# Attention's two heads as pairs of half-array products, in a two-layer decoder trunk on one core

## What is computed

```python
def dilated_branch(q, k, v, rel_bias, window, dilation):      # layer 0, per query group
    ...
    scores = jnp.where(allowed[:, None], scores + bias, NEG_INF)
    m = jnp.max(scores, axis=-1)
    p = jnp.exp(scores - m[..., None])
    l = jnp.sum(p, axis=-1)
    o = jnp.einsum('bdnqhk,bdnkhc->bdnqhc', p, vv.astype(jnp.float32))
```

## Time and profile before

| | |
|---|---|
| median of 3 executions | 1723.69 us (1720.13 to 1725.03) |
| the profiled execution's own time | 1725.31 us |
| its span | 1723.5 us |
| PE busy | 1635.0 us, 95% |
| DVE busy | 1329.4 us, 77% |
| ACT busy | 1119.9 us, 65% |
| POOL busy | 53.0 us, 3% |

### The profile page before, as it was taken

One profiled execution on the slowest core, in us unless ns is written; L12 is line 12 of the kernel. 1 busy time (PEld: TensorE's weight loads), 2 busy tenths in 40 slices (PEclk: granted clock), 3 DMA queues, 4 the chain that ended last, 5 costly groups with the idle time before them and its releaser, 6 DMA issues.

```text
span 1723.5 us, 26169 instructions
## 1 busy us (share of the span) xinstructions
PE 1635.0 (95%) x8684; PEld 1372.9 (80%) x8684; DVE 1329.4 (77%) x1711; ACT 1119.9 (65%) x1498; POOL 53.0 (3%) x37
## 2 busy tenths in 40 slices
PE   7999988999988987999999999999999999999996
PEld 6899957999976765788788788788788787887885
DVE  4777665555557754898898898998998998998995
ACT  5555445334445643787777777777787788787774
POOL 1422100000000000000000000000000000000000
PEclk9999988999998988999999999999999999999999
DMA  9744324666612342899999999998999998998990
GB/s 263 198 122 122 104 86 141 189 183 183 171 37 74 110 172 74 311 378 347 331 380 325 343 372 333 334 383 328 330 386 332 331 385 319 341 384 321 343 379 29
DMA packets 272721, 442.77 MB, mean 257 GB/s; under 512 B 12496, under 2 KB 120160, under 8 KB 272672
## 3 DMA queue, kind: packets, MB, share of 16 engines
q1 hardware_dynamic: 271664, 438.47, 72.7%
q0 software_dynamic: 1008, 3.68, 1.1%
HBM read 440.28 MB, written 1.84 MB: 257 GB/s over the span
## 4 chain that ended last, share of the span: by engine, by line
PE 90%; DVE 5%; ACT 2%; DMA 2%; issue 1%; DVEq 0%; POOL 0%; ACTq 0%; POOLq 0%
PE ps L594 26%; PE ps L595 26%; PE ps L596 26%; PE ps L892 2%; PE ps L903 2%; PE ps L667 2%; DMA big<-in_even_w_in 2%; PE ps L933 1%; DVE w_lo L1253 1%; PE ps L689 1%; PE ps L665 1%; PE ps L676 1%; ACT w_hi L974 1%; PE ps L621 1%; PE ps L693 0%
## 5 line engine op out<-in xcount | busy, mean ns | idle before, releaser
L1253 DVE TENSOR_TENSOR w_lo<-big,w_hi 128x1024 fp32r<-128x1024 f32 (+1 forms) x843 | 991.5, 1216 | 247.6 <-ACT w_hi L974 156.3
L1195 ACT CAST w_hi<-big 128x1024 fp32r<-128x1024 f32 x672 | 689.8, 1056 | 142.6 <-PE ps L596 142.2
L594 PE MATMUL ps<-w_hi,m_hi 128*128 128x512 f32 (+1 forms) x1008 | 400.3, 397 | 4.9 <-DVE w_lo L1253 4.9
L596 PE MATMUL ps<-w_hi,m_lo 128*128 128x512 f32 (+1 forms) x1008 | 391.4, 388 | 0.0
L595 PE MATMUL ps<-w_lo,m_hi 128*128 128x512 f32 (+1 forms) x1008 | 391.3, 388 | 0.0
L594 PE MATMUL ps<-h_hi,w_hi 128*128 128x256 f32 (+1 forms) x824 | 240.7, 292 | 5.4 <-DVE w_lo L1253 5.4
L595 PE MATMUL ps<-h_lo,w_hi 128*128 128x256 f32 (+1 forms) x824 | 236.4, 287 | 0.0
L596 PE MATMUL ps<-h_hi,w_lo 128*128 128x256 f32 (+1 forms) x824 | 236.2, 287 | 0.0
L594 PEld LDWEIGHTS ps<-w_hi,m_hi 128*128 128x128 f32 x1008 | 190.8, 189 | 46.0 <-issue 9.5
L974 ACT CAST w_hi<-big 128x1024 fp32r<-128x1024 f32 (+1 forms) x171 | 165.4, 978 | 95.0 <-PE ps L596 82.0
L596 PEld LDWEIGHTS ps<-w_hi,m_lo 128*128 128x128 f32 x1008 | 190.7, 189 | 39.6
(11 more groups left out here) (202 smaller groups left out, 1424.7 us busy)
## 6 DMA issues: line engine op xcount, KB each, us to landing
big<-in_odd_w_gate SPq DMA_DIRECT2D x112, 1024.0 KB, 7.0
big<-in_odd_w_up SPq DMA_DIRECT2D x112, 1024.0 KB, 7.5
big<-in_odd_w_down SPq DMA_DIRECT2D x112, 1024.0 KB, 6.7
big<-in_even_w_in SPq DMA_DIRECT2D x42, 512.0 KB, 4.6
big<-in_even_w_gate SPq DMA_DIRECT2D x22, 512.0 KB, 3.9
big<-in_even_w_up SPq DMA_DIRECT2D x22, 512.0 KB, 4.0
big<-in_even_w_down SPq DMA_DIRECT2D x22, 512.0 KB, 3.7
big<-in_w_out SPq DMA_DIRECT2D x20, 512.0 KB, 4.3
```

Source lines behind the costliest of these rows:

```text
L594: mm(dst, a[0], b[0], start=start, stop=False, **kw)
L596: return mm(dst, a[1], b[0], start=False, stop=stop, **kw)
L1195: nc.scalar.copy(w_hi[:, slot, :], ring[s][:, (u % 2) * UNIT:(u % 2 + 1) * UNIT]).then_inc(s_hi, 1)
L1253: return V.tensor_tensor(dst, src, lead.bitcast(F32), ALU.subtract)
```

## The change

Both heads' score products are issued in one call, head 0 and head 1 by turns, each on its half of the array's rows (`scores(nxt)`), and both heads' V products in one call, each on its half of the columns (`mix(now)`). Head 1 gets buffers of its own: `zq` for scores (it takes the place of `qiT` and `kiT`), `selm` or `zq` for the turned probabilities, `pr` for the probabilities; its third group of scores goes to the half bank beside head 0's, and DVE reads that bank first (`third_read`), since the next pair's first projection goes there. DVE reads both heads' scores in one place of the step (`head_scores(nxt)`). The order of calls on PE, ACT and DVE is new.

```diff
-        qiT = sb("qiT", [P, 4, SEQ])
-        kiT = sb("kiT", [P, SEQ])
+        zq = sb("zq", [P, 5 * SEQ])
+        qiT = zq[:, 0:4 * SEQ].rearrange("p (c n) -> p c n", c=4)
+        kiT = zq[:, 4 * SEQ:5 * SEQ]
...
+            zs = zq if pair.nbr == NBR and hh else z
...
+        def score_columns(pair, hh, t, b0, b1):
 
             if pair.nbr == 1:
                 n0 = SEQ if pair.cross else P
-                return ps[:, hh, (0, n0)[t]:(n0, n0 + SEQ)[t]].rearrange("p (b s) -> p b s", b=1)
-            if t == 0:
-                return ps[:, 0, 0:NBR * P].rearrange("p (b s) -> p b s", b=NBR)
-            return ps[:, 1:3, :].rearrange("p k n -> p (k n)")[:, 0:NBR * SEQ].rearrange("p (b s) -> p b s", b=NBR)
+                src = ps[:, hh, (0, n0)[t]:(n0, n0 + SEQ)[t]]
+            elif t == 0:
+                src = ps[:, hh, b0 * P:b1 * P]
+            elif b1 <= 2:
+                src = ps[:, (2, 7)[hh], b0 * SEQ:b1 * SEQ]
+            else:
+                src = ps[:, pair.bank(pair.nbr), hh * SEQ:(hh + 1) * SEQ]
+            return src.rearrange("p (b s) -> p b s", b=b1 - b0)
+
+        def value_bank(pair):
+            return ps[:, 5 if pair.l == 0 else 2, 0:SEQ]
+
+        def turned(pair, hh):
+
+            return ps[:, 5 if hh == 0 or pair.kind == "even" else 0 if pair.gs[-1] == NPAIR - 1 else 7, :]
+
+        def probs(pair, hh):
+            if pair.kind == "even":
+                return (pn[:, 0:CAUSAL], pr[:, 0:CAUSAL])[hh]
+            return pr[:, 512 * hh:512 * hh + (512 if pair.cross else CAUSAL)]
+
+        def probs_turned(pair, hh):
+            second = selm[:, :] if pair.kind == "even" else zq[:, 0:512]
+            return (pts[:, :], second)[hh]
...
+                if pair.l == 0 and m == 0 and norm is None:
+                    pe.wait_ge(S["third_read"], PAIRS if pair.cross else pair.g)
...
+            def scores(pair):
+
                 S = s_at[pair.l]
                 pe.wait_ge(S["evacuated"], pair.before() + (1 if pair.cross else pair.nbr + 1))
 
-                if pair.l == 0:
-                    pe.wait_ge(S["scores_read"], 2 * pair.g + hh + 1)
-                elif not (isinstance(pair.g, int) and pair.g == 0):
-                    pe.wait_ge(S["scores_read"], 2 * pair.g + hh)
-                r = slice(HD * hh, HD * hh + HD)
+                pe.wait_ge(S["scores_read"], 2 * pair.g + 1)
                 k = keys(pair)
-                for b in range(pair.nbr):
-                    mm(score_banks(pair, hh, 0)[:, b, :], qT[r, pair.par, b, 0:P], k[r, 0:SEQ if pair.cross else P],
-                       start=True, stop=True)
-                    last = mm(score_banks(pair, hh, 1)[:, b, :], qT[r, pair.par, b, P:SEQ], k[r, :], start=True, stop=True)
-                last.then_inc(S["scores"], 1)
+                if pair.nbr == 1:
+                    turns = [[(0, 0), (1, 0)]] * 2
+                else:
+                    turns = [[(1, 2), (0, 0), (0, 1), (0, 2), (1, 0), (1, 1)], [(1, 0), (0, 0), (0, 1), (0, 2), (1, 1), (1, 2)]]
+                for i in range(len(turns[0])):
+                    for hh in range(2):
+                        t, b = turns[hh][i]
+                        r = slice(HD * hh, HD * hh + HD)
+                        if (hh, b) == (1, 2) and t:
+                            pe.wait_ge(S["third_left"], pair.g + 1)
+                        last = mm(score_columns(pair, hh, t, b, b + 1)[:, 0, :], qT[r, pair.par, b, tok(t)],
+                                  k[r, 0:SEQ if pair.cross or t else P], start=True, stop=True)
+                        if (hh, b) == (0, 2) and t:
+                            last.then_inc(S["third_left"], 1)
+                        if i == len(turns[0]) - 1:
+                            last.then_inc(S["scores"], 1)
...
-            def mix(pair, hh):
+            def mix(pair):
+
                 S = s_at[pair.l]
-                pe.wait_ge(S["probsT"], 2 * pair.g + hh + 2)
-                if hh == 0:
-                    pe.wait_ge(S["mix_lo"], pair.g + 1)
-                    if not pair.cross:
-                        pe.wait_ge(S["values"], pair.g + 1)
-                o = ps[HD * hh:HD * hh + HD, 6, :]
+                pe.wait_ge(S["probsT"], 2 * pair.g + 3)
+                pe.wait_ge(S["mix_lo"], pair.g + 1)
+                if not pair.cross:
+                    pe.wait_ge(S["values"], pair.g + 1)
                 v = (vx[:, pair.l * XPAIRS + pair.gs[0] - PAIRS, :, :] if pair.cross else vN[:, :, :])
-                v = v[:, :, HD * hh:HD * hh + HD]
-                mm(o[:, 0:SEQ], v[:, 0, :], pts[:, 0:SEQ], start=True, stop=False)
-                if pair.cross:
-                    last = mm(o[:, 0:SEQ], v[:, 1, :], pts[:, SEQ:2 * SEQ], start=False, stop=True)
-                else:
-                    last = mm(o[:, P:SEQ], v[:, 1, :], pts[:, SEQ:SEQ + P], start=False, stop=True)
-                last.then_inc(S["mixed"], 1)
+                for t in range(TT):
+                    for hh in range(2):
+                        h = slice(HD * hh, HD * hh + HD)
+                        n0 = 0 if pair.cross else P * t
+                        last = mm(ps[h, 6, n0:SEQ], v[:, t, h], probs_turned(pair, hh)[:, SEQ * t:SEQ * (t + 1) - n0],
+                                  start=(t == 0), stop=(t == TT - 1))
+                        if t == TT - 1:
+                            last.then_inc(S["mixed"], 1)
...
+                p(0)
                 if not now.cross:
                     turn_values(now)
-                if now.kind == "even":
-                    p(0)
-                    scores(now, 1)
-                    p(1)
-                    turn_probs(now, 0)
-                    p(2, 3)
-                    mix(now, 0)
-                    turn_probs(now, 1)
-                    p(4)
-                    scores(nxt, 0)
-                    mix(now, 1)
-                    return
-                scores(now, 1)
-                p(0)
+                p(1)
                 turn_probs(now, 0)
-                p(1, 2)
-                mix(now, 0)
+                p(2, 3)
+                turn_probs(now, 1)
                 if nxt is not None:
-                    scores(nxt, 0)
-                p(3)
-                turn_probs(now, 1)
+                    scores(nxt)
                 p(4)
-                mix(now, 1)
+                mix(now)
...
+                if pair.kind == "even" and hh:
+                    act.wait_ge(S["summed"], 2 * pair.g + 1)
...
                 exps(now, 0)
                 if now.kind == "even":
                     e(0)
+                    values()
                     hi_mat(aft, 0)
                     e(1)
+                    exps(now, 1)
                     hi_mat(aft, 1)
-                    exps(now, 1)
                     probsT(now, 0)
                     e(2)
                     hi_mat(aft, 2)
                     e(3)
+                    probsT(now, 1)
                     hi_mat(aft, 3)
-                    probsT(now, 1)
                     e(4)
                     hi_mat(aft, 4)
                 else:
-                    hi_mat(aft, 0)
-                    outs(hi, now, 0)
                     exps(now, 1)
                     e(0)
+                    values()
+                    outs(hi, now, 0)
                     probsT(now, 0)
-                    outs(hi, now, 1)
+                    hi_mat(aft, 0)
                     e(1)
                     e(2)
+                    probsT(now, 1)
+                    outs(hi, now, 1)
                     hi_mat(aft, 1)
                     hi_mat(aft, 2)
-                    probsT(now, 1)
                     outs(hi, now, 2)
...
+            def head_scores(pair):
 
                 S = s_at[pair.l]
-                n = 2 * pair.g + hh
-                zv, pv, n0 = views(pair, hh)
-                dve.wait_ge(S["scores"], n + 1)
-                if pair.kind == "even" and hh == 0:
+                if pair.kind == "even":
                     dve.wait_ge(s_bm, NBR * pair.g + NBR)
-                tiles = ((0, n0), (n0, n0 + SEQ))
-                for t, (a, b) in enumerate(tiles):
-                    src = score_banks(pair, hh, t)
-                    if pair.cross:
-                        last = V.tensor_scalar(zv[:, :, a:b], src, SCALE, None, ALU.mult)
-                        continue
-                    cols = slice(P, SEQ) if t == 0 else slice(0, SEQ)
-                    add = bmp[:, pair.par, hh, :, cols] if pair.l == 0 else bias[:, bass.ds(n, 1), cols]
-                    last = V.scalar_tensor_tensor(out=zv[:, :, a:b], in0=src, scalar=SCALE, in1=add,
-                                                  op0=ALU.mult, op1=ALU.add)
-                last.then_inc(S["scores_read"], 1)
-                dve.wait_ge(S["scores_read"], n + 2)
-                if pair.kind == "odd":
-
-                    V.tensor_tensor(zv[:, 0, :], zv[:, 0, :], selm[:, :], ALU.add).then_inc(S["masked"], 1)
```

(46 more changed lines are left out.)

41 lines of the change are left out of this document (26 added, 15 removed).

## The result

The changed kernel takes 1676.35 us (median of 4 executions, 1676.01 to 1677.85); the kernel before, on the same chip, 1722.95 (1720.13 to 1725.03). The ratio is 0.9732, 95% interval 0.9715 to 0.9749: 46.6 us less. The profiled execution took 1677.85 us, its span 1676.1, 47.4 less than the span before.

What follows compares the result with a forecast made beforehand. PE was taken to bound layer 0's loop (167.13 of 172.00 us busy). Layer 0's loop -10 and tail -10, layer 1's tail -6.6, loop -3 and first step -2 made -32: 1692 us, range 1680 to 1708.

Steps and rivals of the forecast that it cites:

- The halves run together: Layer 0's step on PE: both heads' scores take 2.3 us for 4.32, a pair's V products 0.9 for 1.6.
- Head 7 against heads 0 and 1 of the indexer: Indexer rows before: two instructions of head 7 alone span 0.59 us, four of heads 0 and 1 on different halves 0.61.
- all saved: V products on the two column halves: the best bound, 0.8 us per pair, against 1.6 with nothing saved.
- The chain that takes over in layer 0: Layer 0, head 0's turning to the next: 18.65 us plus 1.65 from POOL's masks, 20.3 per step; the loop gains 10.
- The tail of layer 0: Layer 0's last steps: 5.7 us from paired calls and the 4.25 us wait lost, nothing for the clock: -10 us.
- Layer 1's loop: Layer 1's steps: between nothing and 1.5 us saved each, taken as 0.5 for six steps: -3 us.
- The waits that I feared: Layer 1's steps: scores wait for the key's copy behind a copy and a cast; first probabilities wait for both heads' score reads.
- The tail of layer 1: Layer 1's last steps: 5.7 from paired calls, wait 4.3 us for 2.98, 2.2 from the half-clock stretch: -6.6 us.
- two fewer calls fall into the half-clock stretch: Layer 1's tail: two calls fewer run at half clock, at twice the price, worth 2.2 us.
- A chain of DVE that makes steps of 21.6 to 21.8 us: Rival, layer 0's loop: DVE's chain is longer and the loop gains nothing; -22, 1702 us; chance 0.16.
- the products don't overlap: Rival: score products run singly in the loop, layer 0's step 22.5 us, tails gain half; -8, 1716 us; chance 0.05.
- a cost per turn to the other half: Rival: each switch of half drains the array, 224 turns at 0.1 us, +22; 1738 us; chance 0.04.

Runs made afterwards that it cites:

- third mask apart: Changed kernel with POOL's masks started after head 0's probabilities of two pairs ago, the third only after head 1's probabilities: 1671.04 us.
- scores apart: Changed kernel with head 0's score products wholly ahead of head 1's and a PE wait on its own last product between them: 1710.87 us.
- casts moved: Changed kernel with the three output-unit casts of step 7 moved behind the last pair's exponentials, in both layers: 1679.53 us.
- V products in series: Changed kernel with head 0's V products written ahead of head 1's by loop order alone, no wait between: 1678.73 us.
- scores in series: Changed kernel with all of head 0's score products written ahead of head 1's by loop order alone, no wait between: 1689.12 us.
- both in series: Changed kernel with score and V products both written one head after the other by loop order alone: 1689.95 us.
- V apart: Changed kernel with head 0's V products ahead of head 1's and a PE wait on its own last product between them: 1689.00 us.
- copies first: Changed kernel with ACT's copies of query and key turnings put ahead of the first weight cast in layer 1's steps: 1682.77 us.
- both apart: Changed kernel with score and V products each one head after the other, with a PE wait on its own last product between: 1727.90 us.

## Why the prediction was right, and where it fell short

Of the 47.4 us of the span the forecast had 32. Most of what it missed is in layer 1: 6.5 us in its loop and 3.7 in its tail.

**The halves run together** (forecast 2.3 us for the scores of a pair, 0.9 for the V products): measured 2.24 and 0.80. Head 7 against heads 0 and 1 of the indexer was the right row to trust. The bound "all saved" held for the column halves too. The Trainium skill, page "TensorEngine Tiling (Array Packing)", section "Key Properties", says that different tiles execute in parallel; the rows agree, to 1.93 times for the scores and twice for V.

**The chain that takes over in layer 0** was right in kind and close in size. Forecast: 18.65 us and 1.65 of POOL's lock, 20.3, with waits of 1.2 and 0.3 us. Measured: a lock of 1.68, a step of 19.94, waits of 0.85 and 0.21. The lock lies on both sums, and not on the split and one sum. The scores are not on the chain, as forecast, but only by 0.2 us. The run with the third mask apart shows that the lock was what bound the step. In all -12.1 for -10.

**The tail of layer 0**: -10.9 for -10, and that it fits is luck. The sum took off the whole wait of 4.25 us, put the new waits at nothing and the clock at nothing. The new waits are there (0.86 and 3.40 us in step 7, 2.27 behind it): in all PE stood still 49.08 - 40.95 = 8.1 us before and 38.22 - 31.41 = 6.8 after, 1.3 less. The low stretch, which was to stay, went from 13.7 to 6.8 us. Half of PE's busy time in it is what the half clock costs, so I estimate 2.5 us for that (10.96 / 2 - 5.94 / 2), and 7.1 are left for the paired calls, which were priced at 5.7.

**Layer 1's loop is the step that failed**, -9.5 for -3. The prediction put it so: "I take 0.5 per step, six steps: -3". Two things are in it. The full steps gained 1.0 us each, 6 x 1.0 = 6: two thirds of the bound of 1.5, and not one third. The waits that I feared are there, 0.74 and 0.55 us, but PE's step before was not work alone. Its timeline in the kernel before has, once in each step:

```profile
572.03 0.65 PE L689 MATMUL ps<-pts,vN 128*64 128x256 f32 x2 [0.57 <-ACT pts L1036]
```

In the loop this wait went away. PE's own work fell from 9.61 - 0.57 = 9.04 to 8.62 - 1.29 = 7.33 us, its waits rose by 0.72 only. The other 3.3 us are step 0: 1.0 as in the other steps, the rest with the clock, which was low for 0.9 us of this step and not for 5.6. It came back 6.8 us after it fell and not 13.5. The prediction had seen that PE runs at half clock there, and priced only one score call by it. With the scores apart the low stretch is 3.4 us longer than with them paired, so the overlap is at least a part of why it is shorter; what else shortened it against the kernel before wasn't tried.

**The tail of layer 1**: -10.3 for -6.6. The wait was sized well (4.3 forecast, 4.16 measured). The term of the clock was not: "two fewer calls fall into the half-clock stretch" counts 2.2 us, but the stretch itself shrank from 17 us to 3.3. Half of PE's busy time in it, 14.81 and 3.30 us, gives 5.8 us by the same estimate. Why the clock came back sooner after a longer wait wasn't tried; with the casts moved, the wait was 0.75 us and the clock didn't fall at all. The last 1.4 us, in the stages behind, go with a clock that was low for 17.1 us in all after the tail and not for 20.5; that was only argued.

**The rivals.** A chain of DVE that makes steps of 21.6 to 21.8 us is ruled out by the step of 19.94. That the products don't overlap was given 1716 us, since the tails would gain by the order alone. Kept apart, the kernel took 1727.9. Its 5 us more for layer 0's loop came out (5.2), and the tails did gain by the order, 1.5 and 4.6 us, but less than it said, and layer 1's loop lost 4.1. Of a cost per turn to the other half nothing is to be seen: 24 records in turns take 2.24 us, 12 in a row 2.16.

## What to carry to other kernels

Price products on disjoint halves of the array at one for two, and then look for the chain that takes over. To switch such an overlap off for a test, put a wait between the two, since turning the loops left all of it for V and about half for the scores. An addition on POOL made a sum or a split of DVE that ran beside it 0.7 to 1.1 us longer, and a maximum not at all, so put it over work for which nothing waits, and count each mask's place by itself. Where the granted clock is low after a long wait of PE, count how long: here the stretches became shorter with the change (13.7 to 6.8, 13.5 to 6.8 and 17 to 3.3 us), and the forecast counted little of that.

## What the runs showed of the hardware

- PE starts a product on a free half ahead of products on the busy half that stand before it in the program. In the V products in series it passed three, and in the scores in series also three, with four of each head side by side.
- A wait of PE on its own last product costs little: 0.13 us per pair of V calls, 0.12 per pair of score calls.
- The granted clock fell inside layer 1's loop only in runs with the scores kept apart, for 3.4 us each time, at a cost of 1.5 us (a step of 10.43 for 8.89). The kernel before has its heads' scores one by one as well, and no such fall. Why is open.
- In the first step of layer 0 PE waits 2.27 us for `pn` in most of these kernels. The clock fell to the lower level for 3.4 us around it in the runs with V, scores and both in series, the casts moved and V apart, and did not in the changed kernel and the runs with scores apart and copies first. (With both apart it fell 4 us ahead of the step.) With V in series the first step, from head 0's turning to the next, took 91.82 - 70.48 = 21.34 us and not 19.94. That is 1.4 us of spread between runs alike in that place.
